# Modulation columns of a five-block transformer kernel: column sums on TensorE replaced by one reducing VectorE instruction for each slot

## The reference, cut to what matters

```
cond = silu(c)
for i in range(4):
    mod = einsum('bd,sde->sbe', cond, ada_w[i]) + ada_b[i]     # ada_w[i]: [2, 1024, 3072]
    shift, scale, gate = split(mod, 3)
    h = x * (1 + scale[0]) + shift[0]
    y = mixer_i(h)
    x = layer_norm(ALPHA * x + (1 + gate[0]) * y, ln_g[i, 0], ln_b[i, 0])
    h = x * (1 + scale[1]) + shift[1]
    y = swiglu(h, ffn_w_in[i], ffn_w_out[i])                   # hidden width 2816
    x = layer_norm(ALPHA * x + (1 + gate[1]) * y, ln_g[i, 1], ln_b[i, 1])
```

## Time and profile before

| | |
|---|---|
| median of 3 runs | 3570.35 us (3568.2 to 3574.76) |
| the profiled execution's own time | 3571.12 us |
| its span, first to last instruction | 3569.1 us |
| PE busy | 3373.3 us, 95% of the span |
| VectorE busy | 1700.5 us, 48% |
| GpSimd busy | 1314.2 us, 37% |
| ScalarE busy | 1218.1 us, 34% |
| DMA | 374.08 MB, mean 105 GB/s |

### The profile page before, as it was taken

The page is one execution under the profiler, slowest core; times in us unless marked ns, Lnnn a source line. Parts: engine busy times, 40 slices in busy tenths (PEclk is TensorE's granted clock), DMA queues, the critical chain, the costliest instruction groups (busy, mean ns, idle before and its releaser), DMA issues.

```text
span 3569.1 us, 43233 instructions
## 1 busy us (share of the span) xinstructions
PE 3373.3 (95%) x15372; PEld 2673.9 (75%) x15372; DVE 1700.5 (48%) x2643; ACT 1218.1 (34%) x1906; POOL 1314.2 (37%) x603
## 2 busy tenths in 40 slices
PE   7987899999989999989999999999999998999998
PEld 6765578886757888767788878767888775668886
DVE  2344545512246554377655343556654347662223
ACT  3246433222234332336432243124332332643322
POOL 3430134443313444430444444433444443024442
PEclk9978999999999999989999999999999998999999
DMA  4310045532212554320455423102554331013332
GB/s 136 106 36 1 24 154 184 186 130 88 77 36 96 198 184 157 103 60 8 147 188 182 142 90 99 44 29 82 202 187 159 109 90 52 1 48 112 94 101 70
DMA packets 102534, 374.08 MB, mean 105 GB/s; under 512 B 11392, under 2 KB 11520, under 8 KB 102272
## 3 DMA queue, kind: packets, MB, share of 16 engines
q1 hardware_dynamic: 102240, 371.77, 31.8%
q0 software_dynamic: 160, 0.52, 0.0%
HBM read 370.15 MB, written 2.10 MB: 104 GB/s over the span
## 4 chain that ended last, share of the span: by engine, by line
issue 44%; PE 41%; POOL 13%; DVE 1%; ACT 1%; DMA 0%; POOLq 0%; SPq 0%; DVEq 0%; ACTq 0%
POOL w_lo L562 12%; PE bank L659 11%; PE bank L661 11%; PE bank L660 11%; PE bank L1092 1%; PE bank L703 1%; PE bank L704 1%; PE bank L705 1%; PE bank L1108 1%; PE bank L1061 0%; PE bank L1001 0%; PE bank L999 0%; PE bank L1000 0%; PE bank L908 0%; PE bank L1134 0%
## 5 line engine op out<-in xcount | busy, mean ns | idle before, releaser
L562 POOL TENSOR_TENSOR w_lo<-raw,w_hi 128x1024 fp32r<-128x1024 f32 x501 | 1226.9, 2455 | 2147.2 <-ACT w_hi L1202 2147.1
L1202 ACT ACTIVATE w_hi<-raw 128x1024 fp32r<-128x1024 f32 x501 | 525.9, 1057 | 1268.9 <-PE bank L661 1054.2
L659 PE MATMUL bank<-h_hi,w_hi 128*128 128x512 f32 x2264 | 888.5, 392 | 15.0 <-POOL w_lo L562 8.2
L661 PE MATMUL bank<-h_hi,w_lo 128*128 128x512 f32 x2264 | 883.1, 390 | 0.0
L660 PE MATMUL bank<-h_lo,w_hi 128*128 128x512 f32 x2264 | 883.1, 390 | 0.0
L659 PEld LDWEIGHTS bank<-h_hi,w_hi 128*128 128x128 f32 x2264 | 426.4, 188 | 109.0 <-POOL w_lo L562 10.7
L661 PEld LDWEIGHTS bank<-h_hi,w_lo 128*128 128x128 f32 x2264 | 426.2, 188 | 89.4
L660 PEld LDWEIGHTS bank<-h_lo,w_hi 128*128 128x128 f32 x2264 | 426.3, 188 | 88.8 <-issue 1.0
L2131 DVE SCALAR_TENSOR_TENSOR ada_acc<-ada_raw,cond,ada_acc 128x1024 f32<-128x1024 f32 x168 | 271.8, 1618 | 236.4 <-DMA ada_raw<-ada 235.2
L659 PE MATMUL bank<-hid_hi,w_hi 128*128 128x512 f32 x880 | 344.4, 391 | 0.0
L661 PE MATMUL bank<-hid_hi,w_lo 128*128 128x512 f32 x880 | 342.5, 389 | 0.0
(11 more groups left out here) (345 smaller groups left out, 4235.0 us busy)
## 6 DMA issues: line engine op xcount, KB each, us to landing
raw<-weights SPq DMA_DIRECT2D x501, 512.0 KB, 3.6
ada_raw<-ada SPq DMA_DIRECT2D x192, 512.0 KB, 4.4
layer_const<-layer_const SPq DMA_DIRECT2D x5, 512.0 KB, 4.6
x<-x_t SPq DMA_DIRECT2D x1, 2048.0 KB, 8.1
y_t<-x SPq DMA_DIRECT2D x8, 256.0 KB, 2.0
tables<-big_const SPq DMA_DIRECT2D x1, 768.0 KB, 8.9
cols<-columns SPq DMA_DIRECT2D x1, 573.5 KB, 9.1
rope_i<-positions POOLq DMA_DIRECT2D x2, 256.0 KB, 4.5
```

Source lines behind the costliest of these rows:

```text
L562: nc.gpsimd.tensor_tensor(w_lo[k % RING][:, :, :], raw[k % RING][:, :, :], w_hi[k % RING][:, :, :].bitcast(F32), ALU.subtract).then_inc(sm ...
L659: mm(out, w_hi[r][:, at, :], hi, start=first and at == 0, stop=False)
L661: op = mm(out, w_lo[r][:, at, :], hi, start=False, stop=last and at == len(pairs) - 1)
L1202: fn(w_hi[t % RING][:, :, :], raw[t % RING][:, :, :], ACT.Copy).then_inc(sm.hi_done, 1)
```

## The change

`ada_w` is laid out in DRAM the other way round: a slot now has 128 results on the partitions and the 1024 input features along the free dimension. The vector c comes as a 128x1024 array in which every partition holds all of it (`cond_row`, in the place of `ada_acc`); ACT takes its silu in place. One VectorE instruction (`tensor_tensor_reduce`) multiplies a slot by `cond_row` and sums along it into one column of `ada_part`. Eight slots still make a group of 1024 results, and VectorE adds the bias without PE. There are as many slots of as many bytes as before, loaded in the same places.

```
-            ada_acc = place("ada_acc", [P, SLOT], F32)
+            cond_row = place("cond_row", [P, D], F32)
...
+            def load_cond():
+                sp.dma_start(cond_row[:, :], cond).then_inc(sm.cond_loaded, 16)
+
             sp.dma_start(kp[:, :], kept).then_inc(sm.const_loaded, 16)
             sp.dma_start(x[:, :, :], xT).then_inc(sm.const_loaded, 16)
             sp.dma_start(co[:, :], cols).then_inc(sm.const_loaded, 16)
+            load_cond()
...
                 load_slots(DT)
+                if part != "first" and at + 1 < len(parts):
+                    load_cond()
                 load_ffn(at + 1 < len(parts))
...  PE
-                def ada_sums(g, i):
-
-                    if not with_ada:
-                        return
-                    pe.wait_ge(sm.ada_used, a + 8 * g + 8 + 8 * i)
-                    for j in range(8):
-                        op = mm(bank[7][:, j:j + 1], ada_acc[:, j * P:(j + 1) * P], ones[:, 0:1], start=True, stop=True)
-                    op.then_inc(sm.ada_sum, 1)
-
-                with pe.Fori(0, 5) as i:
-                    for q in range(8):
-                        m_tile(k + q, mt + q, i, 8, 8, h_hi, h_lo, [8])
-                        if q == 5:
-                            ada_sums(0, i)
-                for q in range(40, 2 * FT - EARLY):
-                    m_tile(k + q, mt + q, 0, 0, 0, h_hi, h_lo, [8])
+                linear(2 * FT - EARLY, h_hi, h_lo, [8])
...  ACT
+            def cond_silu():
+                n.add(cond=1)
+                act.wait_ge(sm.cond_loaded, 16 * n["cond"])
+                fn(cond_row[:, :], cond_row[:, :], ACT.Silu).then_inc(sm.cond_done, 1)
+
-            def squares_beside(slots):
+            def squares_beside(slots, ada=False):
                 for m in range(DT):
                     split_ahead(slots - (m == DT - 1))
+                    if m == 3 and ada:
+                        cond_silu()
...  VectorE
                 def ada_slot(a, kc, i):
                     dve.wait_ge(ada_loaded[a % ADA_RING], 16 * (a // ADA_RING + 1) + 64 * i)
-                    if kc == 0:
-                        op = v.tensor_scalar(ada_acc[:, :], ada_raw[a % ADA_RING][:, :], cond[:, 0:1], None, ALU.mult)
-                    else:
-                        dve.wait_ge(sm.ada_used, a + 8 * i)
-                        op = v.scalar_tensor_tensor(ada_acc[:, :], ada_raw[a % ADA_RING][:, :], cond[:, kc:kc + 1],
-                                                    ada_acc[:, :], ALU.mult, ALU.add)
-                    op.then_inc(sm.ada_used, 1)
+                    w = ada_raw[a % ADA_RING][:, :]
+                    v.tensor_tensor_reduce(w, w, cond_row[:, :], 1.0, 0.0, ALU.mult, ALU.add,
+                                           ada_part[:, kc:kc + 1]).then_inc(sm.ada_used, 1)
 
                 def ada_out(g, i):
-                    dve.wait_ge(sm.ada_sum, cg + g + 1 + i)
-                    v.tensor_tensor(mod[ahead % 2][:, bass.ds(8 * g + 8 * i, 8)], bank[7][:, 0:8],
+                    dve.wait_ge(sm.ada_used, a0 + 8 * g + 8 + 8 * i)
+                    v.tensor_tensor(mod[ahead % 2][:, bass.ds(8 * g + 8 * i, 8)], ada_part[:, :],
                                     co[:, bass.ds(COLS["ada_b"][0] + 48 * ahead + 8 * g + 8 * i, 8)],
                                     ALU.add).then_inc(sm.ada_mod, 1)
+                    dve.wait_ge(sm.ada_mod, cg + g + 1 + i)
```

More of the change, by code:

```diff
@@ L212, in stream_length, with program @@
     return n
-def program(nc, xT, wstream, ada, cols, kept, bigc, layerc, pos, yT, parts):
+def program(nc, xT, wstream, ada, cond, cols, kept, bigc, layerc, pos, yT, parts):
     slots_total = stream_length(parts)
@@ L762, in early_tiles, with residual_tiles @@
                 early_done()
-            def residual_tiles(done, hi, lo, chunks, sums, parts_from=None, after_first=None):
+            def residual_tiles(done, hi, lo, chunks, sums, parts_from=None):
                 k, mt, per = n["slot"], n["mt"], len(chunks)
@@ L1096, in hgrn, with ffn @@
                 values(7)
[L1098 removed]
+            def ffn(sums):
                 early_tiles()
[L1100 to L1120 removed]
+                linear(2 * FT - EARLY, h_hi, h_lo, [8])
+                residual_tiles(0, hid_hi, hid_lo, [8, 8, 6], sums, parts_from=n["part"])
                 n.add(part=FT)
@@ L1179, in _ @@
                     layer_norm(sums_out[0], sums_out[2])
-                ffn(at + 1 < len(parts), None if part == "first" else pivot(sums_down[0]))
+                ffn(None if part == "first" else pivot(sums_down[0]))
                 if part != "first":
@@ L1499, in _ @@
                 if part == "first":
-                    fn(cond[:, :], col("c", 0, 8), ACT.Silu).then_inc(sm.cond_done, 1)
+                    cond_silu()
                     act.wait_ge(sm.gate_pre, 1)
@@ L1554, in _ @@
                 else:
-                    squares_beside(1)
+                    squares_beside(1, ada=at + 1 < len(parts))
                     normed_input()
@@ L2148, in up @@
                                     ALU.subtract).then_inc(sm.part_lo, 1)
-                if ahead is not None and a0 == 0:
-                    dve.wait_ge(sm.cond_done, 1)
+                if ahead is not None:
+                    n.add(cond=1)
+                    dve.wait_ge(sm.cond_done, n["cond"])
                 with dve.Fori(0, 5) as i:
@@ L2284, in ada_stream @@
         return np.zeros((1, P, SLOT), np.float32)
-    return np.stack([w[p, s, c * P:(c + 1) * P, g * SLOT:(g + 1) * SLOT]
-                     for p in layers for s in range(2) for g in range(3) for c in range(DT)])
+    return np.stack([np.ascontiguousarray(w[p, s, :, t * P:(t + 1) * P].T)
+                     for p in layers for s in range(2) for t in range(3 * D // P)])
 def column_pack(a):
@@ L2328 @@
         "x_t": np.ascontiguousarray(a["x"][0].T.reshape(DT, P, S).transpose(1, 0, 2)),
-        "weights": weight_stream(a, PARTS), "ada": ada_stream(a["ada_w_2"], PARTS), "columns": column_pack(a),
+        "weights": weight_stream(a, PARTS), "ada": ada_stream(a["ada_w_2"], PARTS),
+        "cond": np.ascontiguousarray(np.broadcast_to(a["c_2"].reshape(1, D), (P, D))), "columns": column_pack(a),
         "kept_const": kept, "big_const": big, "layer_const": layer,
```

13 lines of the change are left out of this document (4 added, 9 removed).

## The result

The changed kernel takes 3532.55 us in the median of four runs (3521.84 to 3532.93); the kernel before took 3572.56 beside it (3568.2 to 3575.2). The medians differ by 40.0 us, or 1.1%; the ratio worked out over all these runs is 0.988, with a 95% interval from 0.9867 to 0.9893. A second measurement of the same changed kernel gave 3530.3 us (3525.61 to 3534.66) against 3571.86, ratio 0.988 (0.9865 to 0.9896), which is 41.6 us. The forecast was 3528, with a range from 3518 to 3540. The profiled execution took 3521.84 us, 49.3 less than that of before; it is the fastest of its four, and the other three took 3532.45 to 3532.93.

A forecast was written before the change was run, and what follows sets the result against it. PE, busy 95% of the span, was taken as the bound: 3569.1 us of span - 44.4 for the sums + 1.3 at the start = 3526.0, plus 2.0 around the span, gives 3528 us, range 3518 to 3540.

The forecast's parts named there:

- What is removed: PE's column sums in feed-forward stages with modulation: 24 groups at 1.85 us each, 44.4 us removed.
- PE's loop of four tiles: PE's feed-forward loop goes round every 4 tiles instead of 8; a back edge can't cost much.
- The price of the reduction: VectorE's new instruction: T = 1.3 us plus 0.08 a slot, some 0.3 of waiting for GpSimd; covered, cost 0.
- The halving: Skill's rule of half throughput with two non-bf16 SBUF sources: a slot would take about 2.6 us, by the rows 1.4.
- The end of the stage: PE's wait for the last `hid_lo` at the down projection: counted 0, with a bound of 4 x 1 us.
- ACT: Silu and up to two table loads in the output projections of parts 0, 1 and 2: hidden, cost 0.
- The start: `cond_row` queued ahead of the first weight slot delays ACT's first split: +1.3 us, bounds 0 and 2 x 1.3.
- the fourth rival: Part of the gain is lost elsewhere, through the granted clock in mixers and around norms: 3538 to 3555 us, chance 0.06.
- The first rival: Reduction slow at T = 2.6, covered in the loop, PE waits at four stage ends: 3528 to 3552 us, chance 0.12.
- The second rival: Slow reduction and GpSimd's exclusion add up in the loop: 12.5 us a pair, 3656 us, chance 0.03.
- T = 2.1 with full waits: Reduction time from which the second rival decides in the loop, at 11.4 us a pair; without any waits T = 4.4.
- The third rival: No change: PE's pause at the sums has another reason and stays, 45.37 us for eight tiles; 3571 us, chance 0.01.

The follow-up runs named there:

- the kernel with half a reduction more: The changed kernel with one more reduction of 512 columns ahead of each full one, T about 2.0 us: 3533.75 us, ratio 0.9899.
- Two passes: The changed kernel with every slot reduced twice in place, one after the other, standing for T = 2.6 us: 3643.93 us, ratio 1.0201.
- the copies with one SBUF operand: The changed kernel with two copies of 512 columns from the slot into PSUM ahead of each reduction: 3551.55 us, ratio 0.9949.

## Why the prediction was right, and where it was weak

**What is removed.** 24 x 1.85 = 44.4 us stood in the sum. The removal alone gave 44.1, and putting the matmuls back took 43.0. The choice of the pace (1.85) over the record starts (1.70, for 40.8) is borne out by the pair with columns, 12.72 - 10.88 = 1.84 us, in a kernel that differs from the changed one in them and in PE's loop of eight tiles alone.

**PE's loop of four tiles** cost nothing: the pairs at 598.10 and 608.98 lie 10.88 us apart.

**The price of the reduction.** Forecast were T = 1.3 us and 0.08 for the read-out, about 0.3 of blocking. The changed kernel's group by tile (count, then minimum, median and maximum in ns) has

```profile
L2120 DVE CUSTOM_DVE_ANT_0 ada_raw<-ada_raw,cond_row x192: 1209/1226/3437, 473.6 to 2669.0; 128x1024 f32<-128x1024 f32 x192
L2120 DVE DVE_READ_ACCUMULATOR2_ANT ada_part<- x192: 73/77/86, 474.8 to 2670.2; 128x1 f32 x192
```

1.226 and 0.077 us, with a mean of 1.604 in the page, so 0.38 of blocking. I had said that T could hardly be below L2131's 1.29; it is, by 0.06. Twice L1804's 691 ns less one fixed part was the better guide: from 0.69 us for 512 columns (in the kernel with half a reduction more) and 1.226 for 1024 the fixed part comes to about 0.16. The estimate left GpSimd's effect on `hid_lo` where it was, and that is what was found.

**The halving.** The statement of the Trainium skill's page "Vector Engine (DVE) Microarchitecture Reference", section "Points that are easy to get wrong", that two non-bf16 SBUF sources halve the throughput of the scalar-tensor-tensor form would, on L2131's 1.29, have given about 2.6 us, if it covers this instruction. For this product with its sum, both sources fp32 in SBUF, the trace doesn't agree: 1.226 us for 1024 columns, and 0.69 us for 512, in the kernel with half a reduction more, is what L1804 takes with one of the two in PSUM. The Trainium skill's page doesn't name this instruction, and no run shows whether it counts as that form.

**The end of the stage.** I counted 0 with a bound of 4 us. PE never waits for `hid_lo`, and the cover grew from 1.7 to 4.0 us, because VectorE doesn't wait for PE's sums any more; the kernel with the sums alone removed has 3.7 in the same stage.

**ACT.** Hidden, with 0.41 us to spare where I had 0.5.

**The start.** +1.3 us was mis-sized: the first split moved from 12.05 to 12.86, by 0.81. The squares ahead of it on ACT start no later than before, at 10.29 in the changed kernel where it was 10.76. Taking the row out from ahead of the weights gave 1.01 back. This is half a microsecond, and all within one term.

**Sum and median.** The sum was 43.1 us, and the two measurements gave 40.0 and 41.6, while the profiled execution lost 49.3. The two executions of the changed kernel that were profiled lie 12.9 us apart. The view of each core has for the one and for the other:

```profile
core 0: 3519.8 us, clock 0.964
```

```profile
core 0: 3532.7 us, clock 0.961
```

If a mean of 0.964 comes from time at half of 2.4 GHz, that is an estimated 2 x 0.036 x 3519.8 = 253 us at 1.2 GHz; 0.961 is 276 us. PE does in 22 us at the lower level what takes 11 at the upper: by this estimate that is most of the 12.9. Ahead of the second measurement it had been expected that 0.003 less in the mean goes with about 11 us more. The eight executions of the changed kernel bear it out: the one at 0.964 spans 3519.8 us, two at 0.963 span 3523.7 and 3525.3, one at 0.962 spans 3531.3, and four at 0.961 span 3530.5 to 3532.7. The windows show where half of it lies. First the window from 100 to 200 us of the one, then of the other (columns as in the earlier trace rows):

```profile
100.00:200.00 100.00, 99.22 (x443) 73.93 (x441) 33.69 (x40) 27.86 (x32) 45.63 (x20) 0.95 0.32 100
```

```profile
100.00:200.00 100.00, 99.22 (x419) 73.13 (x418) 31.53 (x37) 26.86 (x32) 45.92 (x19) 0.90 0.32 101
```

The granted clock is 0.95 and 0.90 there, and 0.95 and 0.93 in the first 100 us. By the same estimate that is 2 x (0.05 + 0.02) x 100 = 14 us more at 1.2 GHz, so 7 us longer, and the first pair product of "first" comes at 484.13 in the one and at 490.94 in the other. That is over half of the 12.9, between two executions of one kernel. So the differences of a few microseconds around the sum are of the size of this scatter. Whether the earlier stages bring a little more time at the lower level, as the fourth rival has it, is left open; it would be worth some 3 us. Four of the changed kernel's eight executions show a mean of 0.961, and none of the four without the sums does (0.963 and 0.964), which would fit it, but these are too few to tell.

**The first rival's cover, which was wrong.** It said of T = 2.6 "in the loop that is still covered", and gave 3528 to 3552. Two passes measured 3644. The step that failed is "7.7 us a pair, and waits for GpSimd on top": it took the blocking as it is in a VectorE with time to spare. Those waits were 2.4 us a pair in the changed kernel, and with 7.7 that is 10.1, under 10.88; with two passes they were about 4.3. (VectorE's own part was then 7.0 of the 11.30 us, as two passes start 1.25 us apart.) When VectorE comes late, ACT is late with it, splits two slots together, and GpSimd's two turns fall into the row of reductions. This order is read from the timeline; no run delays ACT by itself. Had the reduction taken 2.6 us, as the Trainium skill's statement would have it, the change would have been about 2% slower, and not a little less fast, if two passes stand rightly for one slow one. The 0.12 that I gave the first rival and the 0.03 of the second should have been the other way round.

**The second rival, which had the mechanism.** It forecast 12.5 us a pair and 3656 in all, from two blocked slots of 2.39 us each. Measured were 11.30 to 12.12 a pair and 3644, with 2.1 to 2.2 of blocking each. The total is nearer than the pair's price deserves, and that is luck: once the pace has settled, the loop gives only 3 x 11.30 + 12.12 - 4 x 10.88 = 2.5 us a group, 50 us if all 20 groups of the loops gave it. The rest comes at the stages' beginnings and ends. In the first stage the changed kernel's first five pair products, at 484.13 to 521.94, take 37.8 us, as VectorE catches up with PE there; with two passes, at 490.54 to 540.50, it is 50.0. From first to last product the stage takes 227.3 and 257.1 us: of the 29.8 between them about 12 lie in these first five products, about 9 in the last two distances, in each of which eight reductions stand, and about 9 in the loop between. The four stages make 125 us in all, which is the difference of the two profiled executions (3647.25 and 3521.84); the medians differ by 111. The threshold "T = 2.1 with full waits" is consistent with what was found: 2.0 still holds, 2.5 doesn't. That the collision with GpSimd is what decides is shown by two experiments, which take away GpSimd's turn (pairs at 10.88 again) or VectorE's second SBUF operand (+19 in place of +111). The Trainium skill's page "SBUF — State Buffer", section "SBUF: two separate sides", has the rule: a VectorE instruction with two SBUF inputs and a GpSimd instruction that reads SBUF exclude each other, and the one that starts first holds the other up for its whole length. The trace agrees: with GpSimd's instruction beside them the copies with one SBUF operand kept 0.70 us each, and with two passes the two middle reductions of a pair lost 2.1 to 2.2 of its 2.39 us.

**The third rival** (the pause stays) fell: PE has no pause, and 384 records fewer.

## What to carry to other kernels

Tiny matmuls on a saturated PE cost by their number: eight sums with one column each, 1.85 us, were 24 times on the path, and moving them to an engine with a third of its time free was worth 1.1%. Price such a piece by the pace of the stage with and without it, not by the records. And before calling an engine's extra work hidden, ask what it blocks when it is late: the spare time of VectorE here was 3.4 us a pair, but 2.5 us more of instructions with two SBUF operands already cost 111 us, since both GpSimd instructions of a pair then fell on reductions in full and held VectorE up for 4.3 us a pair, where it had been 2.4. The same time in instructions with one SBUF operand cost 19 us.

## What the runs showed of the hardware

- The product with its sum over two fp32 operands in SBUF ran at 1.226 us for 1024 columns and 0.69 for 512, as fast as with one operand in PSUM, plus 0.077 for the read-out.
- VectorE's instructions with two SBUF operands and GpSimd's subtraction exclude each other instruction by instruction: a reduction of 1.226 us took up to 3.48 beside it (with two passes), and 1.228 at most where GpSimd's instruction was shrunk to one column. With reductions back to back the loss was 2.1 to 2.2 us for each of GpSimd's instructions, 4.3 a pair; in the changed kernel it was 0.73 in the reduction at 595.74 and 1.66 in `hid_lo`, 2.4 a pair. GpSimd's own two instructions stretched from 2.39 each to 6.06 for both. VectorE's copies from SBUF to PSUM kept their 0.70 us beside it.
- Sixteen matmul records of one column (eight matmuls in the program) with 128 rows and columns of weights cost PE 1.84 us, 0.115 us each, though their output was read by nobody.
- A difference of 0.003 in the mean granted clock of one kernel's executions goes with 12.9 us of its 3530.
